# Index products behind the second chunk; the norm of the recurrent output, prompt attention and sample attention interleaved; cache loads begun at the end of the recurrence

## The reference, cut to what matters

```python
dots = jnp.einsum('bthd,bsd->bths', qi, ki) * IDX_DIM ** -0.5
score = jnp.einsum('bth,bths->bts', wi, jax.nn.relu(dots))
score = jnp.where(admissible[None], score, -jnp.inf)
_, sel = lax.top_k(score, topk)
...
logits = jnp.einsum('bthd,btkhd->bthk', q, k_sel) * A_HEAD_DIM ** -0.5
p = jax.nn.softmax(logits, axis=-1)
return jnp.einsum('bthk,btkhd->bthd', p, v_sel)
```

```python
mu = jnp.mean(y, -1, keepdims=True)
var = jnp.mean(jnp.square(y - mu), -1, keepdims=True)
y = ((y - mu) * lax.rsqrt(var + LNX_EPS)).reshape(b, t, W_B) * lnx_g + lnx_b
y = (y + bonus) * g          # g = sigmoid(gl) @ rwkv_g2
```

## Time and profile before

| | us |
|---|---|
| median of 3 runs | 1781.27 (1779.48 to 1789.93) |
| the profiled execution | 1777.66, of which its span 1776.1 |
| layer 0: rows, chunks and index products, 0 to 160.9 | 160.9 |
| layer 0: selection in rounds, 160.9 to 298.7 | 137.8 |
| layer 0: recurrence, 298.7 to 374.5 | 75.8 |
| layer 0: norm of the recurrent output, 374.5 to 401.6 | 27.1 |
| layer 0: prompt attention, 401.6 to 450.8 | 49.2 |
| layer 0: sample attention, 450.8 to 479.7 | 28.9 |
| layer 0: output projection to the second norm, to 891.0 | 411.3 |
| busy over the span: PE, DVE, ACT, POOL | 1300.8, 700.0, 316.8, 206.8 |
| mean granted TensorE clock | 0.833 of full speed |

### The profile page before, as it was taken

The page is one execution under the profiler, slowest core; times in us unless marked ns, Lnnn a source line. Parts: engine busy times, 40 slices in busy tenths (PEclk is TensorE's granted clock), DMA queues, the critical chain, the costliest instruction groups (busy, mean ns, idle before and its releaser), DMA issues.

```text
span 1776.1 us, 23388 instructions
## 1 busy us (share of the span) xinstructions
PE 1300.8 (73%) x8400; PEld 825.2 (46%) x8400; DVE 700.0 (39%) x1412; ACT 316.8 (18%) x714; POOL 206.8 (12%) x239
## 2 busy tenths in 40 slices
PE   5989962955797399995299999368468964989932
PEld 2667752923346244442146677268233462444412
DVE  0236998354024111111803479964521441111126
ACT  1143210213201011111113423011121110111101
POOL 0300060003011200001300003400030112000022
PEclk9989985975896599998599899678678956999975
DMA  5391110005530368885512111100157003878841
GB/s 217 104 403 60 60 38 1 4 1 161 199 131 1 124 248 320 335 327 189 197 53 63 36 60 36 38 2 3 47 154 290 1 1 125 341 300 323 340 166 50
DMA packets 67253, 246.34 MB, mean 139 GB/s; under 512 B 8050, under 2 KB 28690, under 8 KB 58002
## 3 DMA queue, kind: packets, MB, share of 16 engines
q1 hardware_dynamic: 47536, 174.90, 26.7%
q0 software_dynamic: 13424, 47.77, 7.6%
q10 hardware_dynamic: 6194, 22.36, 3.1%
HBM read 194.36 MB, written 52.87 MB: 139 GB/s over the span
## 4 chain that ended last, share of the span: by engine, by line
issue 50%; PE 28%; POOL 7%; DMA 5%; POOLq 4%; DVE 3%; ACT 1%; DVEq 0%; SPq 0%; PEldq 0%; ACTq 0%
PE ps L1140 11%; PE ps L606 6%; PE ps L1157 6%; DMA arena<-in_w_dn 3%; POOL arena L525 2%; PE ps L1081 2%; POOLq L557 1%; POOLq L493 1%; POOL arena L580 1%; DMA arena<-in_wa 1%; POOL arena L558 1%; POOL rows_in L570 1%; POOLq L495 1%; PE ps L1074 1%; POOLq L558 1%
## 5 line engine op out<-in xcount | busy, mean ns | idle before, releaser
L1216 ACT ACTIVATE arena<-ps 128x512 f32<-128x512 f32 (+10 forms) x392 | 172.3, 476 | 846.1 <-PE ps L756 219.5
L623 PE MATMUL ps<-arena 128*128 128x272 f32 x1088 | 260.4, 398 | 0.0
L756 PE MATMUL ps<-arena 64*64 64x64 f32 (+3 forms) x4016 | 158.5, 241 | 107.6 <-DVE arena L1861 92.3
L1140 PE MATMUL ps<-arena 128*128 128x512 f32 x512 | 230.4, 602 | 6.1 <-DMA arena<-in_w_dn 3.7
L623 PEld LDWEIGHTS ps<-arena 128*128 128x128 f32 x1088 | 207.3, 192 | 48.5 <-issue 4.0
L756 PEld LDWEIGHTS ps<-arena 64*64 64x64 f32 x4016 | 143.8, 142 | 121.3 <-DVE arena L1861 92.8
L1140 PEld LDWEIGHTS ps<-arena 128*128 128x128 f32 x512 | 98.1, 193 | 133.5 <-issue 132.7
L1157 PE MATMUL ps<-arena 128*128 128x512 f32 x256 | 119.2, 608 | 19.5 <-DVE arena L2328 19.5
L606 PE MATMUL ps<-arena 128*128 128x512 f32 (+1 forms) x256 | 105.1, 573 | 19.4 <-DMA arena<-in_wa 18.8
L1094 PE MATMUL ps<-arena 128*128 128x512 f32 x256 | 114.1, 607 | 2.0 <-ACT arena L1216 2.0
L1072 PE MATMUL ps<-arena 128*128 128x128 f32 x128 | 27.5, 386 | 110.3 <-POOL arena L525 110.3
(11 more groups left out here) (345 smaller groups left out, 1346.8 us busy)
## 6 DMA issues: line engine op xcount, KB each, us to landing
arena<-in_w_gu SPq DMA_DIRECT2D x32, 2048.0 KB, 7.9
arena<-in_w_dn SPq DMA_DIRECT2D x32, 1024.0 KB, 10.8
arena<-in_wf SPq DMA_DIRECT2D x34, 512.0 KB, 3.4
arena<-rows_in SPq DMA_DIRECT2D x32, 512.0 KB, 3.4
rows_out<-arena ACTq DMA_DIRECT2D x32, 512.0 KB, 5.9
rows_in<-arena POOLq DMA_DIRECT2D x12, 1024.0 KB, 25.1
arena<-in_cache_v POOLq DMA_DIRECT2D x64, 128.0 KB, 2.5
arena<-in_cache_k SPq DMA_DIRECT2D x64, 128.0 KB, 2.6
```

The source lines that it names most:

```text
L623: mm = pe.matmul(ps[:, 2 + 2 * h + n % 2, 0:HALF], m.wf[n % 3][:, c, :], m.xT[:, c, h * HALF:h * HALF + HALF], start=c == 0, stop=c == KC - 1)
L756: mm = pe.matmul(out[q], lhsT[q], rhs[q], start=start, stop=stop, skip_group_check=check)
L1140: mm = pe.matmul(ps[:, 3, :], m.xgT[:, c, :], m.w_gu[k][:, c, :], start=c == 0, stop=c == KC - 1)
L1216: return act.activation(out, in_, ACT.Copy)
```

## The change: what it does

In the projections the order on PE becomes chunks 0, 1, all transposes, 2, sample indexer, loras, index product 3, chunk 3, index product 2, 4, index product 1, 5, sample scores, 6, 7, 8. ACT and DVE follow. `start_selection` now stands behind the mix of chunk 5 and one round of selection stands ahead of that of chunk 6. `block_queries` (the fill of `m.QB`) moves from the start of attention to just before the selection.

After the recurrence, the norm's steps stand between those of prompt attention: head sums, gates, logits(0), logits(1), sums of squares, and then the tiles. ACT copies the gates out of PSUM. DVE's reciprocal is cut in two (`y_rates`, 544 columns each), which stand behind normed(0) and behind masked(2); `y_scaled` stands behind masked(3), and `y_out` behind the samples' maxima. The norm works on 544 columns where it worked on 576. The samples' logits stand ahead of output(3) on PE, and ACT copies them before it copies the prompt's last transposes. SP and POOL wait for the last instructions of the recurrence and no longer for `rw_done`; the output projection waits for `rw_done` also.

```diff
@@ -294,7 +294,7 @@
...
 
 
@@ -311,12 +311,11 @@
...
+    m.s_pTn, m.s_o = ([view(R4 + at + w * k, w) for k in range(2)] for at, w in ((2 * T + 2 * PAST, P), (2368, WA)))
     m.K = [view(at, 2, 4, PAST) for at in (R2, XT0)]
-    m.V = [view(at, 4, NPAGE, WA) for at in (R2 + 4096, R4 + 2560)]
+    m.V = [view(at, 4, NPAGE, WA) for at in (R2 + 4096, R2 + 8192)]
 
 
@@ -413,7 +412,9 @@
...
 
-        sp.wait_ge(s["rw_done"], nth(l, "rw_done", 1))
+        sp.wait_ge(s["rw_mm"], nth(l, "rw_mm", len(RW_PE)))
+        sp.wait_ge(s["rw_a"], nth(l, "rw_a", len(RW_ACT)))
+        sp.wait_ge(s["rw_v"], nth(l, "rw_v", len(RW_DVE)))
...
@@ -642,7 +645,7 @@
         else:
-            pe.wait_ge(s["s_relu"], nth(l, "s_relu", 1))
+            pe.wait_ge(s["job_out"], nth(l, "job_out", 4))
         for h in range(4):
...
@@ -651,7 +654,6 @@
...
 
-        pe.wait_ge(s["job_out"], nth(l, "job_out", 4))
...
@@ -686,8 +688,7 @@
...
         pe.wait_ge(s["lora_act"], nth(l, "lora_act", 1))
-        pe.wait_ge(s["tr_copied"], nth(l, "tr_copied", 6))
-        pe.wait_ge(s["tr_sample"], nth(l, "tr_sample", 2))
+        pe.wait_ge(s["s_relu"], nth(l, "s_relu", 1))
...
@@ -719,19 +720,18 @@
...
         columns(l, 0, 1)
         head_transposes(l, 0)
+        head_transposes(l, 3)
         columns(l, 2)
-        head_transposes(l, 3)
+        sample_indexer(l)
         loras(l)
+        indexer(l, 3)
         columns(l, 3)
-        sample_indexer(l)
+        indexer(l, 2)
         columns(l, 4)
-        indexer(l, 3)
+        indexer(l, 1)
         columns(l, 5)
-        indexer(l, 2)
-        columns(l, 6)
-        indexer(l, 1)
-        columns(l, 7)
         sample_scores(l)
+        columns(l, 6, 7)
...
@@ -956,33 +956,31 @@
...
+    def y_sums(l, src):
+
+        for p in range(2):
+            pe.matmul(ps[:, 4 + p, :], m.const("ones_head"), src[:, p, 0:SEQ], start=True, stop=True)
+        for p in range(2):
+            mm = pe.matmul(ps[:, 6, NS * p:NS * p + NS], m.const("ones_head"), src[:, p, SEQ:T], start=True, stop=True)
+        return mm
+
+    def y_gates(l, bank, part):
+
+        for p in range(2):
+            o = ps[:, bank[p], 0:SEQ] if part.stop == SEQ else ps[:, bank[p], 64 + NS * p:64 + NS * p + NS]
+            mm = pe.matmul(o, m.param("lora")[64:128, 128 * p:128 * p + 128], m.Z[64:128, 6, part], start=True, stop=True)
+        mm.then_inc(s["yn_mm"], 1)
 
...
+                w = P * (i + 1)
+                a = (2 * i + h % 2, w * (h // 2)) if i < 2 else (h, 0)
@@ -1009,14 +1007,26 @@
...
+        pe.wait_ge(s["rw_a"], nth(l, "rw_a", len(RW_ACT)))
+        pe.wait_ge(s["rw_v"], nth(l, "rw_v", len(RW_DVE)))
+        y_sums(l, m.yb).then_inc(s["yn_mm"], 1)
+        y_gates(l, (7, 3), slice(0, SEQ))
+        logits(0)
+        pe.wait_ge(s["gate_out"], nth(l, "gate_out", 1))
+        logits(1)
+        pe.wait_ge(s["yn_in"], nth(l, "yn_in", 1))
+        y_sums(l, m.y2)
+        y_gates(l, (6, 6), slice(SEQ, T))
         pe.wait_ge(s["yn_std"], nth(l, "yn_std", 1))
-        logits(0)
-        for i in range(NT):
-            if i + 1 < NT:
-                logits(i + 1)
-            output(i)
-
-    def sample_attention(l):
+        output(0)
+        logits(2)
+        output(1)
+        logits(3)
+        output(2)
+        sample_logits(l)
+        output(3)
+
+    def sample_logits(l):
@@ -1024,6 +1034,7 @@
...
             pe.wait_ge(s["qb_ready"], nth(l, "qb_ready", 1))
+            pe.wait_ge(s["lg_taken"], nth(l, "lg_taken", 4))
...
@@ -1085,6 +1099,7 @@
...
         pe.wait_ge(s["attn_done"], nth(l, "attn_done", 1))
+        pe.wait_ge(s["rw_done"], nth(l, "rw_done", 1))
...
@@ -1231,30 +1245,29 @@
...
-        head_columns(l, 0)
-        columns(l, 2)
-        head_columns(l, 3)
         act.wait_ge(s["fm_used"], nth(l, "fm_used", 1))
         act.activation(m.Z[0:32, 6, :], m.Z[0:32, 6, :], ACT.Tanh)
         act.activation(m.Z[64:128, 6, :], m.Z[64:128, 6, :], ACT.Sigmoid).then_inc(s["lora_act"], 1)
+        head_columns(l, 0)
+        head_columns(l, 3)
+        columns(l, 2)
+        sample_indexer(l)
         for p in range(2):
             job(l, p, m.ea[:, p, :], ACT.Sigmoid, TP, m.param("w0")[:, p:p + 1])
         for p in range(2):
             job(l, 2 + p, m.aa[:, p, :], ACT.Sigmoid, TP, m.param("a0")[:, p:p + 1])
-        columns(l, 3)
-        sample_indexer(l)
+        relus(l, 3)
         act.wait_ge(s["cum_ready"], nth(l, "cum_ready", 1))
         act.activation(m.ea, m.ea, ACT.Exp, scale=-DECAY)
         act.activation(m.ec, m.en, ACT.Exp, scale=-DECAY)
         act.activation(m.en, m.en, ACT.Exp, scale=DECAY).then_inc(s["exps_ready"], 1)
+        columns(l, 3)
+        relus(l, 2)
         columns(l, 4)
-        relus(l, 3)
+        relus(l, 1)
         columns(l, 5)
-        relus(l, 2)
-        columns(l, 6)
-        relus(l, 1)
-        columns(l, 7)
         sample_scores(l)
+        columns(l, 6, 7)
         columns(l, 8)
@@ -1366,15 +1379,22 @@
...
+
+    def y_norm(l):
+
+        act.wait_ge(s["yn_mm"], nth(l, "yn_mm", 2))
+        for p in range(2):
+            ins = copy(m.gate[:, p, 0:SEQ], ps[:, (7, 3)[p], :])
+        ins.then_inc(s["gate_out"], 1)
         act.wait_ge(s["yn_mm"], nth(l, "yn_mm", 3))
+        copy(m.gate[:, :, SEQ:T], ps[:, 6, 64:64 + 2 * NS].rearrange("p (q t) -> p q t", q=2))
+        for p in range(2):
+            act.activation(m.y2[:, p, 0:SEQ], ps[:, 4 + p, :], ACT.Sqrt, bias=m.const("eps")[:, 1:2], scale=1.0 / 64)
+        act.activation(m.y2[:, :, SEQ:T], ps[:, 6, 0:2 * NS].rearrange("p (q t) -> p q t", q=2), ACT.Sqrt,
+                       bias=m.const("eps")[:, 1:2], scale=1.0 / 64).then_inc(s["yn_std"], 1)
@@ -1430,18 +1450,19 @@
...
+        y_norm(l)
         exps(0)
         for i in range(NT):
             if i + 1 < NT:
                 exps(i + 1)
+            else:
+                for g in range(2):
+                    act.wait_ge(s["s_lg_mm"], nth(l, "s_lg_mm", g + 1))
+                    copy(m.s_lg[g][:, 0:PAST], ps[:, 2 - 2 * g, :])
+                    copy(m.s_lg[g][:, PAST:T], ps[:, 3 - 2 * g, 0:NS]).then_inc(s["s_lg"], 1)
             turned(i)
             output(i)
 
-
-        for g in range(2):
-            act.wait_ge(s["s_lg_mm"], nth(l, "s_lg_mm", g + 1))
-            copy(m.s_lg[g][:, 0:PAST], ps[:, 2 - 2 * g, :])
-            copy(m.s_lg[g][:, PAST:T], ps[:, 3 - 2 * g, 0:NS]).then_inc(s["s_lg"], 1)
@@ -1805,22 +1826,25 @@
...
-        mix(l, 0, 1, 2)
+        mix(l, 0, 1)
+        split_queries(l)
+        mix(l, 2)
         key_squares(l)
-        split_queries(l)
+        sample_sums(l)
         decays(l)
+        scores(l, 3)
+        key_rates(l)
         mix(l, 3)
-        key_rates(l)
-        sample_sums(l)
+        scores(l, 2)
         mix(l, 4)
+        scores(l, 1)
         bonus(l)
-        scores(l, 3)
         mix(l, 5)
-        scores(l, 2)
+        block_queries(l)
+        start_selection(l)
+        select_rounds(1)
         mix(l, 6)
-        scores(l, 1)
-        start_selection(l)
-        select_rounds(2)
+        select_rounds(3)
         conv_d(l, 0)
         key_norms(l)
         chunk_inputs(l)
@@ -1831,9 +1855,8 @@
         lru_input(l)
         select_rounds(1)
         lru(l)
-        select_rounds(3)
         dve.drain().then_inc(s["small_ready"], 1)
-        select_rounds(6)
+        select_rounds(7)
         finish_selection()
@@ -1980,28 +2003,31 @@
...
+    def y_centred(l):
         dve.wait_ge(s["rw_a"], nth(l, "rw_a", len(RW_ACT)))
+        dve.wait_ge(s["yn_mm"], nth(l, "yn_mm", 1))
+        for p in range(2):
+            stt(m.yc[:, p, 0:SEQ], ps[:, 4 + p, :], -1.0 / 64, m.yb[:, p, 0:SEQ], mul, add)
+        stt(m.yc[:, :, SEQ:T], ps[:, 6, 0:2 * NS].rearrange("p (q t) -> p q t", q=2), -1.0 / 64, m.yb[:, :, SEQ:T], mul, add)
         dve.drain()
         tt(m.y2, m.yc, m.yc, mul).then_inc(s["yn_in"], 1)
+
+    def y_rates(l, p):
         dve.wait_ge(s["yn_std"], nth(l, "yn_std", 1))
+        dve.reciprocal(m.y2[:, p, :], m.y2[:, p, :])
+
+    def y_scaled(l):
+        dve.drain()
+        tt(m.yc, m.yc, m.y2, mul)
         dve.drain()
         for p in range(2):
             ts(m.yc[:, p, :], m.yc[:, p, :], m.param("lnxg")[:, p:p + 1], m.param("lnxb")[:, p:p + 1], mul, add)
+
+    def y_out(l):
+        dve.drain()
+        tt(m.yc, m.yc, m.bonus, add)
+        dve.drain()
+        tt(m.yT[:, 2:4, :], m.yc, m.gate, mul).then_inc(s["rw_done"], 1)
@@ -2103,7 +2129,9 @@
...
-    def attention(l):
+    def block_queries(l):
+
+        dve.drain()
         dve.memset(m.QB, 0.0)
         dve.drain()
...
@@ -2119,7 +2148,13 @@
...
-            tt(x, ps[:, 0:4, 0:w], bias.unsqueeze(1).broadcast_to([P, 4, w]), add).then_inc(s["lg_taken"], 1)
+            if i < 2:
+                ins = tt(x.rearrange("p (a b) n -> p a b n", b=2),
+                         ps[:, 2 * i:2 * i + 2, 0:2 * w].rearrange("p b (a n) -> p a b n", n=w),
```

(18 more changed lines are left out.)

56 lines of the change are left out of this document (12 added, 44 removed).

## The result

The changed kernel took 1729.24 us (median of 4 runs, 1726.57 to 1743.66) against 1780.38 us for the kernel before (4 runs, 1778.37 to 1789.93). The ratio is 0.9733, with a 95% interval of 0.9706 to 0.976: 47.5 us less, where 63 were forecast. A second set of runs of the same kernel gave 0.9718. It is faster, as forecast. Put against the forecast, which started from 1781.27 us, the ratio gives 0.9733 x 1781.27 = 1733.7, which lies 19 us above 1715 and just above the top of its range, 1732; the median of 1729.24 by itself lies inside it.

What follows compares the result with a forecast made beforehand. DVE was taken to bound the selection, and a chain through PE, DVE and ACT the attention. 10.6 + 21 = 31.6 us a layer, 63 in two, off 1777.66 gave 1714.5, stated as 1715; range 1702 to 1732.

Steps and rivals of the forecast that it cites:

- The start of the selection: Projections: selection's four copies start at 149.1 instead of 160.89, 11.8 us sooner; net 10.6 us a layer, between 8 and 12.
- the other terms of the sum: Start of selection: 160.89 - 15.3 (two chunks less) + 1 (idle times) + 1 (chunk 5's mix) + 1.5 (blocked queries).
- the front: First head transpose to the selection's four copies: forecast 11.8 us shorter in each layer.
- One sign of the prediction: PE's idle time ahead of DVE's masks, 46.14 us, becomes 35 to 36, as selection starts sooner.
- The selection and the recurrence: Four copies to the recurrence's end: same 17 rounds, with chunk 6's mix now inside them, +1.2 us.
- Rival 2: Selection: starts sooner, but the time returns as DVE waits for PE inside it; only attention's 42 us remain, 1736; chance 0.06.
- Norm and prompt tiles: After the recurrence: tile 0 ready at 391 to 394 instead of 409.36, 15.5 to 18 us sooner.
- rival 1: Interleaved norm and prompt stretch: clock stays down as PE waits for ACT and DVE; 7 us a layer, 1729; chance 0.08.
- Behind the keys: Samples' logits done at 437.5, then 21.2 us to the output projection at 458.7 instead of 479.65; 21 us a layer gained.
- Rival 4: Key loads: longer issue interval than 1.65 us; 1.0 us more loses all 31.6 us, 3 us an issue gives 1800; chance 0.03.
- The output weights: `wout`, ahead of the output projection: issued at about 444, lands 12.5 us later at 456.5, 2 us to spare.
- rival 3: Output projection: `wout` lands late; 6 us slower loading costs both layers 4 us each, 1723; chance 0.04.

Runs made afterwards that it cites:

- the filled wait: Changed kernel with eleven useless PE products between the two sets of transposes in each layer, keeping PE busy while it waits for ACT; 1721.40 us, ratio 0.966.
- The kernel with wide loads: Changed kernel with the second group's sixteen key loads replaced by eight of four neighbouring pages each, fixed addresses, no page look-up; 1717.32 us, ratio 0.9646.

## Why the prediction was right in direction and too large

**The start of the selection: the step that failed.** The prediction said of PE's idle times ahead of the samples' scores that two "may grow: the second transposes now wait for ACT's copies behind its tanh and sigmoid, and the loras for the samples' relus", took "0 to 4 us in all, and 1", and against that let the idle time ahead of the loras go. The first of the two was the right place and the wrong size. PE's three idle times up to chunk 3 are 7.94 us where one of 5.29 stood, and 4.3 us of slower products stand behind the first: some 7 us a layer where the term had 1. The wait could have been read from ACT's rows: two table loads of 1.28 us and two activations of 0.68, 4.0 us, stand ahead of the copies, and the same four instructions are what the loras waited 5.29 us for before. The clock behind it was worth 2.9 and 4.4 us in the filled wait. With the four instructions moved, chunk 3 begins 29.2 us behind the first transpose, where unchanged idle times give 29.3, and the copies come 59.8 us behind it, where the prediction had 60.1: the other terms of the sum held together. One of them was off by itself: from the samples' scores on PE to the copies 4.6 us pass, where it had 4.0. Over both layers the front missed by 12.3 us. That is as much as the profiled execution's whole miss of its 1714.5 (12.1). One sign of the prediction was no test of this step: PE's idle time ahead of the masks came to 35.74 us, near its 36, though the selection began 6 us later than forecast. The masks came only 4.7 us sooner than before (293.99 and 298.66), and PE's work ahead of the idle time ended 5.7 us later (258.25 and 252.52).

The Trainium skill, "ScalarE: Activation LUTs", section on what a table load costs, gives 1283 ns and then about 1380 ns of drain, 2.66 us for each switch. The load agrees (1.28 us); the drain doesn't show here, where tanh starts at 91.92, 1.30 us behind the load's start. With the page's figure the four instructions would be an estimated 6.7 us (two switches and two activations of 0.68), by the rows they are 4.0.

**The selection and the recurrence** kept their length but for the 1.2 us of the mix that moved in: 2.1 and 1.6 us longer together. Rival 2, the whole gain lost there, was wrong.

**Norm and prompt tiles** were better than forecast. Tile 0 is normalised 15.1 us behind the recurrence's end (output(0) at 386.05), where 17 to 19 were forecast; rival 1, a clock under 0.65 in the interleaved stretch, was wrong (0.72 from 390.0 to 428.8). But this brought PE to the first group 4 to 6 us sooner behind the recurrence's end than forecast, while the last keys came 58 us behind it, as forecast: PE's wait was 4.81 us where 0 to 4 were forecast.

**Behind the keys.** Layer 0 gained 23.3 us, layer 1 16.7, at 21 forecast and 19 to 23 allowed. The prediction had the logits of the second group at 3.9 or 5.6 us by the clock, yet it priced the last tile behind them at one duration only, 6.2 us, from a trace in which no wait for the keys stood ahead of it. This is the second term that was mis-sized, in layer 1 alone. There, behind 5.51 us of wait, the second group and the tile took 7.1 + 8.4 us, 4 us more than in layer 0, and the value products 1.6 more. The kernel with wide loads shows the whole of it: 77.0 us in both layers. Rival 4, a longer interval of issue, did not come: 52.65 us as before.

**The output weights** (rival 3) came at the edge as written, 12 and 13.5 us after their issue: PE's idle time ahead of the output projection is 1.18 and 0.97 us, where it is 0.94 in kernels that don't wait for them, and ACT's last copy ended 0.1 us before it in layer 1. They cost 0.2 us in layer 0; moving the last tile takes them off.

The sum by stretches of the trace, measured minus forecast: front +6.2 and +6.1; selection and recurrence +0.9 and +0.4; attention -2.3 and +4.3; the rest, where nothing was changed, -4.0; together +11.8 before rounding. The last term is stray between profiles and not merit. Without it the changed stretches brought 47.5 us of 63.
